# Key and value projections as one product, indexer query groups between the key steps, masks and table edges on GpSimd

## The chip, the cores and the metric

One core of a Trainium2 chip runs the whole program in one launch. The metric is the device time of the run in microseconds (us). The kernel before: 1031.42 us, median of 3 runs (1030.24 to 1037.22).

## The reference

One inference step of a transformer layer for a prompt of 512 tokens and a sample of 32 tokens that sees 512 cached ones; the model width is 1024.

```python
h = rmsnorm(x, g_attn)
qa, ka, va, qb, kb, vb, iq, ik, iw, ga, gb = split(h @ w_in)
# a: window attention over chunks c-2..c, with a sink per head, 8 heads on 2 key heads
oa = softmax([qa @ ka.T / 8 + bias, sink]) @ va
# b: sparse attention: an indexer scores all keys, the best of them are attended to
score = sum_h iw[h] * relu(iq[h] @ ik.T) * scale
sel = top_k(score, 128 for the prompt, 136 for the sample)
ob = softmax(qb @ kb[sel].T / 8 + bias) @ vb[sel]
x = x + (sigmoid(ga) * (oa @ w_branch_a) + sigmoid(gb) * (ob @ w_branch_b)) @ w_out
x = x + moe(rmsnorm(x))        # 32 experts of 512, two per token
x = x + sigmoid(rmsnorm(x) @ w_ple_gate) * (p @ w_ple)
y = rmsnorm(x)
# outputs: y, and the new ka, va, kb, vb, ik of prompt and sample
```

`bias` is a T5 relative position table, turned into one row per distance (a Toeplitz table).

## The kernel before

The program is written engine by engine: each engine has its own list of instructions, and semaphores (`x.wait_ge(sem, n)`, `.then_inc(sem, n)`) are all that orders them between engines. SyncE (`sp`) issues nearly all DMAs, in program order, on one queue; GpSimd (`pool`) stores the new keys and values. The stages around the change, in TensorE's order:

1. The normed rows are turned (L900) and VectorE scales them with `g_attn` into hT, 8 planes of 128 features by 544 tokens (512 prompt, 32 sample).
2. Indexer queries: `project` (L881) multiplies slab 0, the 512 indexer columns of `w_in`, by hT in four groups `('iq', m)` of 128 columns, in full f32. In the profile one such product appears as two instructions: 64 products are x128.
3. Indexer keys and head weights: `by_token` (L888), five token tiles, 72 columns, into two narrow PSUM slots, which VectorE copies out (L1894, L1896). The keys are turned (L920 for the prompt, L925 and L926 for the sample).
4. Dots (L940 for the prompt's blocks 1 to 3, eight heads each; L936 for the sample). ScalarE applies the relu (L1522) and VectorE sums over the heads (L1914, L1917).
5. Key and value projections, branch b, then branch a (L952): each of five token tiles is 24 products of 256 columns. Between them stand `sums` (L959), which adds up the sample's four partial scores, and the transposes of the keys (L964, L969, L970).
6. Attention queries `qb` and `qa` (L980): four groups of 48 products each, 272 columns.
7. Attention over 80 units (`scores_of_two`, L1014, and on), from which the later stages follow: merge, output, routing, experts, the last gate.

From step 5 on, a product with f32 accuracy is made of three single-pass ones (fp32r): an operand v is split into a high part (`high`, ScalarE, L1490, a copy rounded to fp32r) and a low part, v minus high (`low_of` L743, `low` L758, GpSimd), and the product is high x high + high x low + low x high. `hT_f` and `hT_lo` are the parts of hT. `sw_high` and `sw_split` count the high and low parts of weights, `f_high` and `f_split` those of hT.

PSUM is shared by two rings, `WIDE` (three slots of two banks) and `NARROW` (two slots of one bank). A list gives the order of their uses and the engine that reads each out; `open_slot` makes TensorE wait for the use three (or two) before, `close` makes the reader wait for TensorE.

Slab 0 holds the indexer weights and later the `qb` weights. Slab 1 is loaded in pieces: `slab_ikw` (indexer keys) and `slab_kva` both start at its beginning, `slab_kvb` lies in its second half, and the `qa` weights fill it at the end. So the load of `slab_kva` waits for the last reader of `slab_ikw`.

SyncE's order is: x, three gains, the bias table's inputs, slabs iq, ikw and kvb, the caches, the constants; then, after `tabp_ready`, the write of the spread bias table to DRAM (`toeplitz<-arena`, 3 MB); then slab `qb` after the last indexer query, slab `kva` after the prompt's indexer keys are turned, slab `qa` after the last of branch a's projections, and ten loads that bring the table back as `toep_a`, `toep_b`, `toep_sa` and `toep_sb`.

VectorE picks the highest scores, eight at a time (`next_eight` L1933, `take_eight` L1937, which overwrites what it took with TAKEN): 16 rounds for each prompt block, 10 for the sample before attention. `mask` (L1944) writes -BIG where a score isn't TAKEN. Behind the selection VectorE writes the edges of the tables: two strips of `toep_a` that no query may see (L1959, L1960) and the sinks (L1961, L1963). Then it clears four PSUM columns (L1966, L1967) after the last attention query was evicted, and `toep_ready` lets attention start.

Of the kernel before, what the change touches and what calls it, by code (L numbers as in the profile page):

```python
# [32 lines left out]
P = 128  # L33
# [14 lines left out]
KV = 2  # L48
# [28 lines left out]
CONSTS = 6  # L77
# [44 lines left out]
def ring(uses, slots):  # L122
# [23 lines left out]
    + [(('kvb', t), 'act') for t in range(TILES)] + [(('kva', t), 'act') for t in range(TILES)], 2)  # L146
# [78 lines left out]
def _program(nc, A, ctx):  # L225
# [53 lines left out]
    for lo, hi in ((0, 16), (16, 24), (24, 32), (32.5, 40.5), (40.5, 48.5), (48.5, 56.5), (68.5, 73), (80, 97), (97.25, 114.25)):  # L279
        twin(arena, "front", int(lo * 256), int(hi * 256))  # L280
# [34 lines left out]
    hT_lo = at(114.25, [KD, NT])  # L315
    score = hb[:, 0:3 * (PAST + NS)].rearrange("p (b n) -> p b n", b=3)
# [23 lines left out]
    kv_hi = {'b': at(32.5, [KD, 256]), 'a': at(40.5, [KD, 256])}  # L340
# [133 lines left out]
    consts_in, gains_in = sem("consts_in"), sem("gains_in")  # L474
# [64 lines left out]
    def _(sp):  # L539
# [7 lines left out]
        for n, g in enumerate(['g_attn', 'g_ffn', 'g_ple']):  # L547
            load(gains[:, n, :], A[g][0].rearrange("(p c) -> p c", c=KD), gains_in)
# [19 lines left out]
        load(sink_in[:, :], A['attn_sink'].to_broadcast([P, HEADS]), consts_in)  # L568

        sp.wait_ge(tabp_ready, 1)  # L570
# [145 lines left out]
    def _(pool):  # L716
# [32 lines left out]
        pool.wait_ge(sw_high, 1)  # L749
        low_of(slab_kvb, slab_kvb, kv_hi['b'], "front").then_inc(sw_split, 1)  # L750

# [8 lines left out]
        pool.wait_ge(sw_high, 2)  # L760
        low(slab_kva, kv_hi['a'], "front").then_inc(sw_split, 1)

# [6 lines left out]
        query_weights_low(3, slab[0], qb)  # L769
        pool.wait_ge(narrow_out['act'], NARROW[('kvb', 4)].out)  # L770
# [3 lines left out]
        pool.wait_ge(narrow_out['act'], NARROW[('kva', 4)].out)  # L774
# [5 lines left out]
        link(pool.memset(toep_sb[:, :, 0:PAST - WIN], 0.0))  # L780
        link(pool.memset(ones, 1.0))

        query_weights_low(7, slab[1], qx)

        def spread_inverse(s):

# [1653 lines left out]
```

## Time and profile before

| what | before |
|---|---|
| median of 3 runs | 1031.42 us (1030.24 to 1037.22) |
| the profiled execution's own time | 1036.8 us |
| its span | 1035.0 us |
| mean granted clock of TensorE | 0.967 of full |
| TensorE busy | 925.9 us |
| VectorE busy | 378.2 us |
| ScalarE busy | 256.5 us |
| GpSimd busy | 132.4 us |

The profile is of one execution, and its span leaves 1.8 us of that execution's time out. Starts are counted from the span's start. "PE" is TensorE, "DVE" VectorE, "ACT" ScalarE, "POOL" GpSimd, "SPq" SyncE's queue of DMA issues; L940 is line 940 of the kernel. The span of an issue ends when it is handed over, not when its data has landed; the DMA view gives the time to landing. The granted clock is a share of 2.4 GHz, so 0.5 is 1.2 GHz.

### The profile page before, as it was taken

To read this page: it belongs to the slowest core of one execution; us is meant where nothing else is said; L and a number is where in the kernel's file an instruction comes from. 1 tells how busy PE (TensorE), PEld (TensorE's weight loads), DVE (VectorE), ACT (ScalarE), POOL (GpSimd) and SP (SyncE) were. 2 spreads that over 40 slices of the span, in tenths; PEclk is the share of its full clock that TensorE was granted. 3 is DMA by queue.
4 is the path that set the end of the run, shared out by engine and by line. 5 is a ranking of instruction groups with operands and counts; after the bars stand their busy time and mean duration, and the time that the engine had idled before them with its cause. 6 is when DMAs were issued, how large, how long until landed. Compare 5 with 4: busy or idle time off the path is not lost.

```text
span 1035.0 us, 14155 instructions
## 1 busy us (share of the span) xinstructions
PE 925.9 (89%) x5699; PEld 591.2 (57%) x5702; DVE 378.2 (37%) x974; ACT 256.5 (25%) x523; POOL 132.4 (13%) x136
## 2 busy tenths in 40 slices
PE   7989999999999999998999977877887888887996
PEld 7869995456999998994333322322322222234775
DVE  4179996764233436453111101101101011102796
ACT  6244326764323233221000000000000000001542
POOL 2403701113030000001111110011010110000000
PEclk9999998999999999997999999999999899999998
DMA  9850602002834316366999999999999999996601
GB/s 265 118 152 2 203 1 62 1 2 68 263 105 120 78 46 244 128 236 239 427 427 425 427 428 428 424 428 425 429 426 426 427 426 425 427 428 264 254 22 66
DMA packets 60132, 263.72 MB, mean 255 GB/s; under 512 B 11054, under 2 KB 36030, under 8 KB 46224
## 3 DMA queue, kind: packets, MB, share of 16 engines
q1 hardware_dynamic: 54160, 250.99, 63.0%
q0 software_dynamic: 5296, 9.79, 2.6%
q10 hardware_dynamic: 624, 2.23, 0.6%
q8 instruction: 36, 0.59, 0.2%
q14 instruction: 16, 0.13, 0.0%
HBM read 253.99 MB, written 16.85 MB: 262 GB/s over the span
## 4 chain that ended last, share of the span: by engine, by line
PE 63%; DMA 29%; DVE 4%; ACT 2%; issue 1%; SPq 1%; DVEq 0%; ACTq 0%
DMA arena<-in_w_up 25%; PE ps L1111 13%; PE ps L1278 12%; PE ps L980 5%; PE ps L1143 4%; PE ps L1426 4%; PE ps L1303 3%; PE ps L881 3%; PE ps L952 3%; DMA arena<-in_w_ple 2%; PE ps L1044 2%; PE ps L1014 2%; PE ps L1065 2%; PE ps L1399 1%; PE ps L1172 1%
## 5 line engine op out<-in xcount | busy, mean ns | idle before, releaser
L1278 PE MATMUL ps<-arena,hT 128*64 128x512 f32 x960 | 234.5, 641 | 39.4 <-DMA arena<-in_w_up 39.2
L1278 PEld LDWEIGHTS ps<-arena,hT 128*64 128x64 f32 x960 | 71.6, 141 | 199.3 <-issue 149.4
L2211 DVE TENSOR_TENSOR xf<-xf,ps 128x256 f32<-128x256 f32 x32 | 13.5, 421 | 401.6 <-ACT xf L1699 379.1
L1111 PE MATMUL ps<-arena_merge,arena_merge 128*128 128x256 f32 x624 | 99.7, 287 | 0.0
L1303 PE MATMUL ps<-arena,xf 128*64 128x512 f32 x336 | 76.7, 598 | 12.8 <-DVE xf L2214 12.8
L1111 PEld LDWEIGHTS ps<-arena_merge,arena_merge 128*128 128x128 f32 x624 | 87.4, 188 | 0.0
L836 POOL DMA_INDIRECT expert_rows<-xf,arena x32 | 32.2, 1007 | 425.6 <-ACT xf L1703 399.8
L1111 PE MATMUL ps<-xf_merge,arena_merge 128*128 128x256 f32 x480 | 82.0, 288 | 0.0
L1699 ACT ACTIVATE xf<-ps 128x256 f32<-128x256 f32 x30 | 11.6, 385 | 259.1 <-PE ps L1278 259.1
L1111 PEld LDWEIGHTS ps<-xf_merge,arena_merge 128*128 128x128 f32 x480 | 69.3, 188 | 0.0
L1703 ACT ACTIVATE xf<-ps 128x512 f32<-128x512 f32 x30 | 17.9, 598 | 159.8 <-PE ps L1303 159.8
L1303 PEld LDWEIGHTS ps<-arena,xf 128*64 128x64 f32 x336 | 24.3, 136 | 50.8 <-issue 43.0
L1143 PE MATMUL ps<-arena_merge,arena_merge 128*128 128x256 f32 x304 | 49.0, 286 | 1.2 <-DVE arena_merge L2045 1.0
L1303 PE MATMUL ps<-hT,xf 128*64 128x512 f32 x176 | 40.2, 598 | 6.6 <-DVE xf L2214 5.2
L1426 PE MATMUL ps<-arena_gate,hT_gate 128*128 128x512 f32 x192 | 44.4, 391 | 1.1 <-ACT arena L1741 0.6
L1143 PEld LDWEIGHTS ps<-arena_merge,arena_merge 128*128 128x128 f32 x304 | 42.9, 191 | 2.5 <-DVE arena_merge L2045 2.0
L980 PE MATMUL ps<-xf_merge,arena_front 128*128 128x272 f32 x256 | 42.9, 289 | 0.0
L2045 DVE TENSOR_TENSOR arena_merge<-arena,arena_merge 128x256 fp32r<-128x256 f32 (+2 forms) x34 | 39.9, 1228 | 5.1 <-ACT arena_merge L1490 5.0
L1490 ACT ACTIVATE arena_merge<-arena 128x256 fp32r<-128x256 f32 (+3 forms) x43 | 37.1, 919 | 16.2 <-DMA arena<-in_w_branch_a 7.2
L1426 PEld LDWEIGHTS ps<-arena_gate,hT_gate 128*128 128x128 f32 x192 | 35.8, 188 | 9.1 <-ACT arena L1741 1.0
L980 PEld LDWEIGHTS ps<-xf_merge,arena_front 128*128 128x128 f32 x256 | 36.2, 189 | 0.0
L1559 ACT ACTIVATE hT<-ps 128x256 f32<-128x256 f32 (+3 forms) x64 | 25.0, 394 | 21.9 <-PE ps L1044 21.2
(309 smaller groups left out, 1311.1 us busy)
## 6 DMA issues: line engine op xcount, KB each, us to landing
arena<-in_w_gate SPq DMA_DIRECT2D x30, 2048.0 KB, 29.4
arena<-in_w_up SPq DMA_DIRECT2D x30, 2048.0 KB, 37.0
arena<-in_w_down SPq DMA_DIRECT2D x11, 2048.0 KB, 36.4
hT<-in_w_down SPq DMA_DIRECT2D x11, 2048.0 KB, 36.5
arena<-in_w_down SPq DMA_DIRECT2D x20, 1024.0 KB, 32.2
arena<-in_w_in SPq DMA_DIRECT2D x10, 1024.0 KB, 6.2
arena<-in_w_in SPq DMA_DIRECT2D x3, 2048.0 KB, 10.5
arena<-in_w_gate SPq DMA_DIRECT2D x8, 512.0 KB, 9.0
```

Source lines behind the costliest of these rows:

```text
L836: pool.indirect_dma_start(ys, bass.IndirectOffsetOnAxis(ap=of, axis=0), src, None, bounds_check=row_bound, oob_is_err=False).then_inc(s, 16)
L881: mm = pe.matmul(w[:, a * 512:a * 512 + HALF], lhs(c), hT[:, c, a * HALF:(a + 1) * HALF], start=c == 0, stop=c == KD - 1)
L952: mm = pe.matmul(ps[0:ROWS[t], 6 + slot, 0:256], rounded(st[:, c, tok(t)]), rounded(mv[:, c, :], "front"), start=c == 0 and k == 0, stop=c ...
L980: mm = pe.matmul(w[:, a * 512:a * 512 + HALF], rounded(st, "front"), rounded(mv[:, c, a * HALF:(a + 1) * HALF]), start=c == 0 and k == 0, ...
L1111: mm = pe.matmul(w[:, 2 * lo_t:lo_t + hi_t], rounded(st[:, c, cols]), rounded(mv[:, c, lo_t:hi_t]), start=c == 0 and k == 0, stop=c == pla ...
L1143: mm = pe.matmul(w[:, q * QW:(q + 1) * QW], rounded(st[t // 2][:, t % 2, m, :]), rounded(mv[:, m, :]), start=m == 0 and k == 0, stop=m == ...
L1278: mm = pe.matmul(ps[g * BLK:(g + 1) * BLK, 2 + s, :], xsT[:, c, col:col + BLK], expert_columns(k, slice(0, 2), c, g), start=c == 0, stop=c ...
L1303: mm = pe.matmul(ps[g * BLK:(g + 1) * BLK, 6 + s, :], hidT[s][:, c % 2, c // 2 * BLK:(c // 2 + 1) * BLK], dn_at(k, c)[:, g * 512:(g + 1) * ...
L1426: mm = pe.matmul(w[:, cols], rounded(st[:, c, :], "gate"), rounded(mv[:, c, cols], "gate"), start=c == 0 and k == 0, stop=c == KD - 1 and ...
L1490: return act.activation(rounded(dst, stage), src, ACT.Copy)
L1559: act.activation(pT_sb[k2][:, j % 2, 0:tiles, j // 2 % 2, :], ps[:, 4 + u % 2, 0:tiles * P].rearrange("p (k n) -> p k n", n=P), ACT.Copy)\
L2045: return dve.tensor_tensor(rounded(v, stage), v, rounded(hi, stage).bitcast(F32), ALU.subtract)
```

## The change

- Indexer queries: group 0 stays in full f32. Groups 1, 2 and 3 are made of three single-pass products, with the weights' high parts `iq_hi` (ScalarE, three instructions, ahead of kvb's) and low parts (GpSimd, in place in slab 0). TensorE's order becomes: group 0, indexer keys, group 1, the prompt's keys turned, group 2, the sample's keys turned, group 3, dots.
- ScalarE waits for slab `kva` and splits it between the sample's indexer keys and group 3's eviction; before, it did so after the dots.
- SyncE issues slab `kva` after the last indexer key tile, ahead of slab `qb`. The gains `g_ffn` and `g_ple` move from the program's start to behind the constants, ahead of the table write.
- Branch a's and b's key and value columns become one product of 512 moving columns: 5 tiles of 24 instead of twice 5 of 24. All four transposes follow the last tile. ScalarE copies each tile in two halves, and the high parts of the `qb` weights are made ahead of these copies.
- `sums` stands behind the second tile, and ScalarE copies it out instead of VectorE.
- The masks of the prompt's blocks 1 to 3 are written by GpSimd (`selected` counts VectorE's finished blocks), block 1's after the qb parts, block 2's after the stores, block 3's after the qa parts.
- The table edges and sinks are written by GpSimd, after block 2's mask and ahead of the qa weights' low parts. Attention's start waits for both GpSimd and VectorE (`toep_ready` 2), ScalarE's first exp for four masks.

```diff
-    [(('xT', t), 'dve') for t in range(TILES)] + [(('iq', m), 'dve') for m in range(4)]
-    + [(('ikT', s), 'dve') for s in 'ps']
-    + [(('dots', b, h), 'act') for b in BLOCKS for h in range(KV if b == 's' else HEADS)] + [('sums', 'dve')]
+    [(('xT', t), 'dve') for t in range(TILES)] + [(('iq', 0), 'dve'), (('iq', 1), 'dve'), (('ikT', 'p'), 'dve')]
+    + [(('iq', 2), 'dve'), (('ikT', 's'), 'dve'), (('iq', 3), 'dve')]
+    + [(('dots', b, h), 'act') for b in BLOCKS for h in range(KV if b == 's' else HEADS)] + [('sums', 'act')]
...
+        sp.wait_ge(narrow_full, NARROW[('ikw', 4)].fill)
+        load(slab_kva, w_in[:, :, C_KVA:C_KVA + 256], slab_in['kva'])
         sp.wait_ge(wide_full, WIDE[('iq', 3)].fill)
         load(slab[0], w_in[:, :, C_QB:C_QB + 512], slab_in['qb'])
-        sp.wait_ge(wide_full, WIDE[('ikT', 'p')].fill)
-        load(slab_kva, w_in[:, :, C_KVA:C_KVA + 256], slab_in['kva'])
-        sp.wait_ge(narrow_full, NARROW[('kva', 4)].fill)
+        sp.wait_ge(narrow_full, NARROW[('kv', 4)].fill)
         load(slab[1], w_in[:, :, C_QA:C_QA + 512], slab_in['qa'])
...
+        mask(2)
+        pool.wait_ge(toep_moved, 16 + 16 * 10)
+        pool.wait_ge(consts_in, 16 * CONSTS)
+        pool.wait_ge(masks_ready, 3)
+        link(pool.memset(toep_a[0:CHUNK, :, TW - CHUNK:TW], -BIG))
+        link(pool.memset(toep_a[CHUNK:P, :, 0:CHUNK], -BIG))
...
+        pool.sem_inc(toep_ready, 1)
         link(pool.memset(ones, 1.0))
 
-        query_weights_low(7, slab[1], qx)
+        query_weights_low(10, slab[1], qx)
+        mask(3)
...
+        def index_queries(m):
+            w = wide(open_slot(WIDE, ('iq', m), wide_out))
+            pe.wait_ge(f_split, KD)
+            for k in range(3):
+                if k == 2:
+                    pe.wait_ge(sw_split, m)
+                for c in range(KD):
+                    st = slab[0][:, c, m * P:(m + 1) * P] if k == 2 else iq_hi[m][:, c, :]
+                    mv = hT_lo if k == 1 else hT_f
+                    for a in range(2):
+                        mm = pe.matmul(w[:, a * 512:a * 512 + HALF], rounded(st, "front"),
+                                       rounded(mv[:, c, a * HALF:(a + 1) * HALF]),
+                                       start=c == 0 and k == 0, stop=c == KD - 1 and k == 2)
+            mm.then_inc(wide_full, 1)
...
+        pe.wait_ge(sw_split, 5)
+        for t in range(TILES):
+            slot = open_slot(NARROW, ('kv', t), narrow_out)
+            for c in range(KD):
+                for k, (st, mv) in enumerate(((hT_f, kv_hi2), (hT_f, kv_lo2), (hT_lo, kv_hi2))):
+                    mm = pe.matmul(by_half(ps[0:ROWS[t], 6 + slot, :]), rounded(st[:, c, tok(t)]), rounded(mv[:, :, c, :], "front"),
+                                   start=c == 0 and k == 0, stop=c == KD - 1 and k == 2)
+            mm.then_inc(narrow_full, 1)
+            if t == 1:
+                sample_sums()
...
+        index_queries(0)
+        index_queries(1)
+        index_keys('p', 0, NP)
+        index_queries(2)
+        index_keys('s', NP, PAST + NS)
+        act.wait_ge(slab_in['kva'], 16)
+        high(kv_hi['a'], slab_kva, "front").then_inc(sw_high, 1)
+        index_queries(3)
```

ScalarE from the high parts of hT to the dots' relus, before. `xf_merge` are hT's high parts, `arena_front<-arena` splits a weight slab, `64x544` evicts half a group of indexer queries, `128x512` and the second `128x544` the indexer keys, `hT<-ps` is a relu.

```order
L1490 ACTIVATE xf_merge_68<-hT 128x544 x8
L1490 ACTIVATE arena_front_81<-arena 128x2048
L1503 ACTIVATE arena_front_85<-ps 64x544 x8
L1507 ACTIVATE arena_front_83<-ps 128x512
L1507 ACTIVATE arena_front_83<-ps 128x544
L1522 ACTIVATE hT<-ps 128x256 x8
```

The same place in the changed kernel, with the same names.

```order
L1537 ACTIVATE xf_merge_68<-hT 128x544 x8
L1537 ACTIVATE arena_front_84<-arena 128x1024 x3
L1537 ACTIVATE arena_front_80<-arena 128x2048
L1553 ACTIVATE arena_front_83<-ps 64x544 x4
L1558 ACTIVATE arena_front_81<-ps 128x512
L1553 ACTIVATE arena_front_83<-ps 64x544 x2
L1558 ACTIVATE arena_front_81<-ps 128x544
L1537 ACTIVATE arena_front_80<-arena 128x2048
L1553 ACTIVATE arena_front_83<-ps 64x544 x2
L1582 ACTIVATE hT<-ps 128x256 x8
```

Three weight splits stand ahead of kvb's, and kva's split (the second `128x2048`) now stands ahead of the last group's eviction; before it stood behind all relus.

SyncE around the table write, before. `128x8x512` is slab qb, then qa; `128x8x256` is slab kva.

```order
L541 DMA g_fin<-in_g_final 128x1024
L541 DMA sink_in<-in_attn_sink 128x8
L541 DMA toeplitz<-arena 2048x1x384
L541 DMA arena<-in_w_in 128x8x512
L541 DMA arena<-in_w_in 128x8x256
L541 DMA arena<-in_w_in 128x8x512
L541 DMA arena<-toeplitz 128x8x256 x2
```

And in the changed kernel.

```order
L543 DMA g_fin<-in_g_final 128x1024
L543 DMA sink_in<-in_attn_sink 128x8
L543 DMA gains<-in_g_ffn 128x8
L543 DMA gains<-in_g_ple 128x8
L543 DMA toeplitz<-arena 2048x1x384
L543 DMA arena<-in_w_in 128x8x256
L543 DMA arena<-in_w_in 128x8x512 x2
L543 DMA arena<-toeplitz 128x8x256 x2
```

Slab kva comes right behind the table write, ahead of slab qb, and two gain loads stand ahead of the write.

## Rows read from the trace of the kernel before

**Rows 1.** the page: the chain that ended last, share of the span by engine.
```profile
PE 63%; DMA 29%; DVE 4%; ACT 2%; issue 1%; SPq 1%; DVEq 0%; ACTq 0%
```

**Rows 2.** the chain of waits, 20 to 161 us: start, length, engine, line, count.
```profile
20.68 29.53 PE ps L881 x128
50.20 8.23 PE ps L888 x80
...
58.95 0.64 PE ps L920 x4
...
60.95 0.74 DVE arena_front L1900
61.73 0.52 PE ps L940 x2
...
79.63 14.31 PE ps L952 x120
...
111.99 48.51 PE ps L980 x384
160.52 0.62 ACT arena L1549
```

**Rows 3.** ScalarE's timeline: start, length, line, operation, count.
```profile
20.56 4.49 ACT L1490 ACTIVATE xf_merge<-hT 128x544 fp32r<-128x544 f32 x8 [3.56 <-DVE hT L1856]
24.96 1.89 ACT L1490 ACTIVATE arena_front<-arena 128x2048 fp32r<-128x2048 f32 x1
28.24 1.25 ACT L1503 ACTIVATE arena_front<-ps 64x544 fp32r<-64x544 f32 x2 [1.39 <-PE ps L881]
```

**Rows 4.** SyncE's queue: start and length of each issue.
```profile
4.08 0.44 SPq L541 DMA_DIRECT2D gains<-in_g_ple  x1
...
25.37 0.68 SPq L541 DMA_DIRECT2D toeplitz<-arena  x1
...
50.24 0.57 SPq L541 DMA_DIRECT2D arena<-in_w_in  x1
...
59.61 0.54 SPq L541 DMA_DIRECT2D arena<-in_w_in  x1
...
111.14 13.15 SPq L541 DMA_DIRECT2D arena<-toeplitz  x10
```

**Rows 5.** DMA issues in 25:26, 50:52, 59:60, us to landing; the packets of 50:52.
```profile
toeplitz<-arena SPq DMA_DIRECT2D x1, 3072.0 KB, 33.7
...
DMA packets 132, 0.20 MB, mean 101 GB/s; under 512 B 0, under 2 KB 132, under 8 KB 132
...
arena<-in_w_in SPq DMA_DIRECT2D x1, 2048.0 KB, 14.4
...
arena<-in_w_in SPq DMA_DIRECT2D x1, 1024.0 KB, 7.7
```

**Rows 6.** the chain, the kernel's last product, 512 columns moving.
```profile
1003.86 21.81 PE ps L1426 x96
```

**Rows 7.** GpSimd's timeline.
```profile
22.03 10.42 POOL L743 TENSOR_TENSOR arena_merge<-hT,xf_merge 128x544 fp32r<-128x544 f32 x8 [19.13 <-DVE arena L1878]
...
121.43 10.07 POOL L758 TENSOR_TENSOR arena_front<-arena,arena_front 128x512 fp32r<-128x512 f32 x8 [5.24 <-ACT arena_front L1490]
```

**Rows 8.** VectorE's timeline: mask, sample's copy, selection's end, last edge row.
```profile
97.66 0.29 DVE L1944 TENSOR_SCALAR arena<-hT 128x256 bf16<-128x256 f32 x1
97.87 0.70 DVE L1955 COPY xf<-ps 32x544 f32<-32x544 f32 x1
...
158.37 0.70 DVE L1937 MATCH_REPLACE8 xf<-nrm,xf 32x544 f32<-32x544 f32 x1
...
160.44 0.67 DVE L1963 TENSOR_SCALAR arena<-sink_in 32x2 f32<-32x2 f32 x4
```

**Rows 9.** windows: busy time by engine, granted clock, DMA share, GB/s.
```profile
62.00:66.00 4.00, 3.94 (x19) 3.71 (x19) 3.58 (x10) 2.87 (x8) 0.00 (x0) 0.59 0.96 333
...
165.00:170.00 5.00, 4.94 (x17) 2.11 (x17) 2.88 (x14) 3.48 (x17) 1.98 (x2) 0.51 0.58 145
```

More of the change, by code:

```diff
@@ L145 @@
     [('table', 'dve')] + [(('ikw', t), 'dve') for t in range(TILES)]
-    + [(('kvb', t), 'act') for t in range(TILES)] + [(('kva', t), 'act') for t in range(TILES)], 2)
+    + [(('kv', t), 'act') for t in range(TILES)], 2)
 UNITS, GROUP_OF, GROUP_UNITS, SET_OF, SET_LAST = [], [], [], [], []
@@ L767, in query_weights_low, with mask @@
                 low(s[:, 4:8, m * P:(m + 1) * P], q_hi(dst, m, 1), "front").then_inc(sw_split, 1)
-        query_weights_low(3, slab[0], qb)
-        pool.wait_ge(narrow_out['act'], NARROW[('kvb', 4)].out)
+        query_weights_low(6, slab[0], qb)
+        def mask(b):
+            _, keys, sc = block_score(b)
+            m0, _ = MSK[b]
+            pool.wait_ge(selected, b)
+            pool.tensor_scalar(msk[:, m0:m0 + keys], sc, TAKEN, -BIG, ALU.is_gt, ALU.mult).then_inc(masks_ready, 1)
+        mask(1)
+        pool.wait_ge(narrow_out['act'], NARROW[('kv', 4)].out)
         for nm, c in (('new_k', 0), ('new_v', P)):
@@ L909, in _ @@
         pe.wait_ge(wide_out['dve'], WIDE[('xT', 4)].out)
-        for m in range(4):
-            slot = open_slot(WIDE, ('iq', m), wide_out)
-            project(slot, lambda c: slab[0][:, c, m * P:(m + 1) * P], P, None, 0).then_inc(wide_full, 1)
+        slot = open_slot(WIDE, ('iq', 0), wide_out)
+        project(slot, lambda c: slab[0][:, c, 0:P], P, None, 0).then_inc(wide_full, 1)
         pe.wait_ge(slab_in['ikw'], 16)
@@ L1495, in _, with index_queries @@
             high(hT_f[:, c, :], hT[:, c, 0:NT]).then_inc(f_high, 1)
+        act.wait_ge(slab_in['iq'], 16)
+        for m in range(1, 4):
+            high(iq_hi[m], slab[0][:, :, m * P:(m + 1) * P], "front").then_inc(sw_high, 1)
         act.wait_ge(slab_in['kvb'], 16)
         high(kv_hi['b'], slab_kvb, "front").then_inc(sw_high, 1)
-        for m in range(4):
+        def index_queries(m):
             w = wide(close(WIDE, ('iq', m), wide_full))
@@ L1523, in _ @@
                 n += 1
-        act.wait_ge(slab_in['kva'], 16)
-        high(kv_hi['a'], slab_kva, "front").then_inc(sw_high, 1)
-        for br, dst, past in (('b', kbT, PAST), ('a', kaT, WIN)):
-            kv_n = kv_b if br == 'b' else kv_a
-            for t in range(TILES):
-                slot = NARROW[('kv' + br, t)].slot
-                act.wait_ge(narrow_full, NARROW[('kv' + br, t)].fill)
-                act.activation(kv_n[0:ROWS[t], t, :], ps[0:ROWS[t], 6 + slot, 0:256], ACT.Copy)\
-                    .then_inc(narrow_out['act'], 1)
+        act.wait_ge(slab_in['qb'], 16)
+        query_weights_high(slab[0], qb)
+        for t in range(TILES):
+            slot, r = close(NARROW, ('kv', t), narrow_full), ROWS[t]
+            act.activation(kv_b[0:r, t, :], ps[0:r, 6 + slot, 256:512], ACT.Copy)
+            act.activation(kv_a[0:r, t, :], ps[0:r, 6 + slot, 0:256], ACT.Copy).then_inc(narrow_out['act'], 1)
+            if t == 1:
+                w = wide(close(WIDE, 'sums', wide_full))
+                act.activation(score_s[0:NS, :], w[0:NS, 0:PAST + NS], ACT.Copy).then_inc(wide_out['act'], 1)
+        for br, dst, past in (('b', kbT, PAST), ('a', kaT, WIN)):
             w = wide(close(WIDE, ('k' + br + 'T', 'p'), wide_full))
@@ L1879, in _, with index_queries @@
         dve.memset(msk, 0.0)
-        for m in range(4):
+        def index_queries(m):
             w = wide(close(WIDE, ('iq', m), wide_full))
@@ L1941, in mask @@
             m0, _ = MSK[b]
-            for lo in range(0, P, 32) if b == 's' else (0,):
+            for lo in range(0, P, 32):
                 ins = dve.tensor_scalar(msk[lo:lo + rows, m0:m0 + keys], sc, TAKEN, -BIG, ALU.not_equal, ALU.mult)
```

107 lines of the change are left out of this document (55 added, 52 removed).

## The prediction, made before the changed kernel ran

> **What bounds the kernel now.** I read the page's chain first: TensorE holds 63% of it, and where it is not TensorE it is mostly a DMA [rows 1]. The change touches the first 165 us alone, so I followed the chain of waits through them [rows 2]. The reader is to see one unbroken TensorE path: indexer queries (L881, 29.53 us), indexer keys (L888, 8.23), a short relay over ScalarE and VectorE that ends at 60.95 + 0.74, the dots from 61.73, the first of two key and value products at 79.63 (L952, 14.31 for 120 products; the second is as long), the attention queries from 111.99 (L980, 48.51), and attention after 160.52. All later stages, expert weights included, are started by TensorE's own progress, so what is won or lost before 160 us should arrive at the end whole. Then I read the three other engines for slack, and SyncE's queue, because the change moves a load past another one [rows 4, 5].
>
> **Indexer queries: what TensorE saves.** Before, one of four groups costs 29.53 / 4 = 7.38 us [rows 2]. Three groups now become 48 single-pass products each. The same shape (272 columns, 128x128 weights) runs in L980 at 48.51 / 384 = 0.126 us [rows 2], so a group costs 6.06 and three save 3 x 1.32 = 4.0 us of TensorE time.
>
> Against that stands a small stall. ScalarE now makes three high parts of the indexer weights before it evicts group 0. It is at 25.05 when f_high is done [rows 3]; three parts of 1024 elements at half of 1.89 bring it to 27.9, the key/value part (1.89) to 29.8, the eviction (1.25) to 31.0 [rows 3], and VectorE's two subtractions (0.74 each by the row of 60.95) to 32.6. VectorE takes the key tiles only after that, and with two slots TensorE's third tile waits about 1.5 us. So group 0 ends at 28.1, the keys at 28.1 + 8.2 + 1.5 = 37.8, and three groups (18.2) with two sets of transposes (0.64 each) end at 57.3. GpSimd's low parts are in time: 22.03 + 10.42 = 32.45 for hT, then 1.25 per 512 elements [rows 7], so 2.5 us per group, the first at 35, needed at 41.8, the last at 40, before its group starts.
>
> **Indexer queries: what sets the end.** TensorE's saving would let the dots start at 57.3 + 1.25 + 1.48 + 0.1 = 60.1 to 60.4, against 61.73: 1.3 to 1.6 us earlier. It does not get that far. ScalarE now waits for slab kva and splits it (1.89) ahead of evicting group 3; the load is issued after the last key tile, at 38, into SyncE's queue behind the bias table's write to DRAM. That write was issued at 25.37 and took 33.7 us to land, at 59.1 [rows 4, 5]. The queue does not overtake: the 2 MB load issued at 50.24 took 14.4 us, until 64.6, and of the 132 packets seen in 50 to 52 us none was of 2 KB, the size of its rows; all are the table's 1.5 KB [rows 4, 5]. After the write it needed 64.6 - 59.1 = 5.5 us, and the 1 MB load behind it (59.61 + 7.7 = 67.3) 2.7 more [rows 4, 5].
> The Trainium skill (DMA: Bandwidth & Descriptors, Queues, rings and completion order) says that descriptors of one ring are consumed in ring order; the trace agrees by the 132 packets. It adds that completion isn't ordered over a queue, which would let kva land early only on engines done with the table.
>
> In the changed kernel the two gain loads (0.44 and 0.45; row of 4.08) stand ahead of the table write, so it goes out at 26.3 and lands at 60.0; kva lands at 60.0 + 2.7 = 62.7. ScalarE: split until 64.6, eviction of group 3 until 65.9; VectorE's subtractions until 67.4; dots at 67.5. That is +5.8 us against 61.73. TensorE idles from 57.3 for 10 us, and its 4 us of saving and the 1.5 us stall both vanish in it. Bounds: if the load slips through, -1.5; if it lands with the slowest ring and a further delay, +7.
>
> TensorE's clock is the second price. After a stretch with little TensorE work 62 to 66 shows 0.59 and then full speed, while 165 to 170 is at 0.51 [rows 9]: the 1.2 GHz level. The dots paid this before as well, and VectorE's sums paced them, so I add nothing; the upper bound is the rival below. The skill (TensorE: Matmul & The Clock Gate, What's actually happening) says that the 1.2 GHz level follows an idle spell and ends with sustained work; rows 9 agree, and by that rule too nothing is added unless the gaps in the dots hold it down.
>
> **Joined key and value product.** 240 products of 256 columns (2 x 14.31 = 28.6 us) become 120 of 512. The nearest row is the kernel's last product: 21.81 / 96 = 0.227 us at 512 columns [rows 6], so 27.3 us: -1.3. No loss of one product's fixed cost would give 0, so the bounds are -1.4 and 0. The second ScalarE copy ahead of the transposes costs 0.3, and a wait between the two branches goes, 0.2. Taken: -1.3. Splitting the qb weights (eight ScalarE parts) moves ahead of the copies, but lies in the 5 us before the first tile is full.
>
> **Masks, sums and edges.** VectorE drops three masks (0.21 from the first to the next row, about 0.8 in all), the sums copy (0.74) and the edges (159.1 to 161.1) [rows 8]. In the old trace the edges ended 0.2 us after ScalarE's first half of the last eviction (160.52 + 0.62) and before the second [rows 2, 8]: hidden. Gone, they win nothing, since attention waits for that eviction. They do give cover: VectorE's selection, shifted by +5.8 - 1.5, ends at 163.4, before the new end of qa at 165.
> On GpSimd seven edge instructions now stand ahead of the low parts of the qa weights and wait for the last bias table load. Those loads were issued from 111.14 to 124.3 [rows 4]; the last are small and land within the 7.7 us of a 1 MB load [rows 5], by 132.0 at the latest; the new ones follow the join's end, +3.3, so 135.3. The edges cost 2 us by VectorE's rows (159.1 to 161.1), 8.8 by GpSimd's 1.25 each [rows 7, 8]; small as they are I take 2.5. The first qa part (2.5) is then ready by 140.3 at the latest, and TensorE wants it at 67.5 + 17.9 + 31.1 + 24.3 = 140.8 (dots 61.73 to 79.63; join to queries 32.4 - 1.3; half of 48.51). Cost 0; with 8.8 for the edges it would be 5.8 late, which is the upper bound. The last mask comes after these parts, but VectorE's selection of block 3 is the later one, and attention wants it at 165.
>
> **Sum.** +5.8 - 1.3 + 0 = +4.5 us. On the profiled execution (1036.8) that gives 1041.3; on the median of the runs, 1031.4, it gives 1035.9. About 1% (10 us) is what a measurement of this kernel can tell from no change, so this is a small loss inside it.
>
> **The rivals.**
> A. The kva load isn't held by the table write, or lands on early rings by 52, so the reordered indexer pays: -1.5 and -1.3, so 1028.6. For it: rings finish at different times, and 1 MB is small. Against it: no large packet in 50 to 52 us [rows 5].
> B. Slower by more than 1%: after 10 us without work TensorE comes back at 1.2 GHz and the gappy dots hold it there. Place: 67 to 86 us. Dots and the sample's part take 17.9 us with the clock back after some 4 us; with it low throughout, about half as much more, +8; if it also catches 5 us of the joined product, +2.5. Time 1031.4 + 4.5 + 8 = 1044. It decides if the clock is still at 0.5 beyond 73 us. For it, 165 to 170 [rows 9]; against it, 66 us, where it came back although VectorE paced the dots.
> C. GpSimd is late: edges cost 8.8 us, or the table's copies land later, and TensorE waits at the qa weights, up to 5.8 us by the bound above; taken at 3: 1039.
> D. The main story holds, but TensorE's 512-column products gain nothing: 1037, inside the forecast.
>
> **How the numbers follow.** Forecast with D 0.66, A 0.18, B 0.07, C 0.07, anything else 0.02. The range for 8 in 10 runs from near A's value to C's and past: 1028.5 to 1041. Only B gives more than +1%, and A gives less than -0.3%; for a deeper gain no row speaks. Faster by over 1% 0.03, within 1% 0.90, slower by over 1% 0.07.
>
> **What would show it.** Right: slab kva lands near 62 to 63 us; ScalarE's wait ahead of the second 2048-element split ends with a DMA; TensorE's dots start at 67 to 68 after 10 us idle; the indexer groups take 6.1 us; L1002 takes 27.3 us for 120; qa starts without a wait; its last eviction starts 4 to 5 us later than at 160.52. Wrong: dots before 62 us, a kva load that took under 15 us, a wait of TensorE for GpSimd near 140, or a late stage whose length changed.

## The result, and the profile after

The changed kernel takes 1046.06 us, median of 4 runs (1044.94 to 1046.73), against 1031.08 us, median of 4 runs of the kernel before (1030.24 to 1037.22). The ratio of the runs on record is 1.0114 (95% interval 1.008 to 1.0148), the plain quotient of the two medians 1.0145; by either it is slower, by 1 to 1.5%. The forecast was 1035.9, range 1028.5 to 1041.

The two medians need one remark. The kernel before scatters: three of its first four runs lie near 1030.8 and one at 1037.2, and of 25 runs in a later job the median is 1036.36 (1028.91 to 1037.78). Against those the changed kernel is 9.7 us slower. The profiled executions, 1036.8 us before and 1045.66 us after, differ by 8.9 us, and so do their spans, so the traces are compared at 8.9.

The page of the changed kernel: span, busy time by engine, and the chain that ended last by engine.

```profile
span 1043.9 us, 14025 instructions
...
PE 927.7 (89%) x5627; PEld 587.8 (56%) x5630; DVE 377.5 (36%) x963; ACT 259.1 (25%) x527; POOL 146.2 (14%) x149
...
PE 59%; DMA 31%; DVE 4%; ACT 3%; issue 1%; SPq 1%; DVEq 0%; ACTq 0%
```

TensorE is busy 1.8 us longer, and DMAs now hold 31% of the chain, 29% before [rows 1]. The new share is one load in the first 65 us: 23.1 of 1043.9 us are 2.2%. The chain of the changed kernel (start, length, what), with lines that answer to [rows 2]:

```profile
32.64 7.25 PE ps L914 x48
...
39.91 23.12 DMA arena<-in_w_in
...
63.05 1.91 ACT arena_front L1537
...
70.85 0.50 DVE hT L1980
...
87.64 11.33 PE ps L1002 x48
...
100.00 16.88 PE ps L1002 x72
...
119.73 48.51 PE ps L1027 x384
...
169.90 0.51 PE ps L1061 x4
```

L914 are key tiles 3 to 5, L1537 ScalarE's split of slab kva, L1980 VectorE's first weighted sum of the dots, L1002 the joined product, L1027 the attention queries, L1061 attention. The reader is to see the 23.12 us of a load in the middle. TensorE works on indexer groups 1 to 3 beside it for the first 20 us and then stands idle until the dots:

```profile
67.72 2.97 PE L984 MATMUL ps<-arena_front,arena_front 128*128 128x256 f32 x12 [7.55 <-DVE arena_front L1945]
```

The joined product starts at 87.64, 79.63 before: +8.0. The queries start at 119.73, 111.99 before: +7.7. Attention starts at 169.90 and 162.06: +7.8.

SyncE's queue and the landing of slab kva, which answer to [rows 4, 5]:

```profile
26.26 0.68 SPq L543 DMA_DIRECT2D toeplitz<-arena  x1
39.91 0.57 SPq L543 DMA_DIRECT2D arena<-in_w_in  x1
...
arena<-in_w_in SPq DMA_DIRECT2D x1, 1024.0 KB, 23.1
```

The load goes out at 39.91 and lands 23.1 us later, at 63.0. Alone behind a free queue a load of this size lands in about 6 us (run e2_table_behind_kva below).

VectorE between the last subtraction of indexer group 3 and the first weighted sum: the four copies together, the first of them by itself, and the same four in the trace before:

```profile
66.21 1.46 DVE L1945 TENSOR_TENSOR arena_front<-ps,arena_front 64x544 fp32r<-64x544 f32 x2 [9.24 <-ACT arena_front L1553]
67.69 2.74 DVE L1971 COPY nrm<-x_nat 32x2 f32<-32x2 f32 x4
...
67.69 1.89 DVE L1971 COPY nrm<-x_nat 32x2 f32<-32x2 f32 x1
...
61.59 0.66 DVE L1905 COPY nrm<-x_nat 32x2 f32<-32x2 f32 x4
```

The four copies of 32x2 take 2.74 us; before they took 0.66. They were not all slowed: the first took 1.89 us, until 69.58, the second and third 0.16 each, as before, and the fourth 0.49.

GpSimd's work that is new or moved, to be read against [rows 7, 8]:

```profile
65.04 4.52 POOL L749 TENSOR_TENSOR arena_front<-arena,arena_front 128x2048 fp32r<-128x2048 f32 x1 [21.45 <-ACT arena_front L1537]
...
105.79 1.11 POOL L782 TENSOR_SCALAR arena<-hT 128x256 bf16<-128x256 f32 x1 [6.18 <-DVEq L2018]
...
126.00 1.50 POOL L782 TENSOR_SCALAR arena<-hT 128x384 bf16<-128x384 f32 x1 [0.70 <-DVEq L2018]
137.40 0.52 POOL L799 MEMSET arena<- 64x512 f32 x1 [9.89 <-DMA arena<-toeplitz]
...
140.43 10.06 POOL L769 TENSOR_TENSOR arena_front<-arena,arena_front 128x512 fp32r<-128x512 f32 x8
150.57 1.95 POOL L782 TENSOR_SCALAR arena<-hT 128x512 bf16<-128x512 f32 x1
```

The low part of slab kva runs from 65.04 to 69.56: VectorE's first copy ended 0.02 us behind it. The masks take 1.11, 1.50 and 1.95 us, the seven edge instructions and their waits 2.8 us (137.40 to 140.19). The first two low parts of the qa weights end near 143.0, and TensorE wants them near 144.0, when half of its 48.5 us from 119.73 are over: a spare of 1 us.

Granted clock (the first number behind the five busy times) in the changed kernel, at the key tiles, the dots and attention's start:

```profile
34.00:37.00 3.00, 3.00 (x20) 3.00 (x19) 0.36 (x2) 0.00 (x0) 3.00 (x3) 0.63 0.91 103
37.00:40.00 3.00, 3.00 (x21) 2.67 (x21) 0.45 (x3) 0.00 (x0) 3.00 (x2) 0.50 0.89 101
...
70.00:74.00 4.00, 2.83 (x11) 2.47 (x10) 3.74 (x9) 1.92 (x5) 1.05 (x2) 0.50 0.15 35
...
170.00:175.00 5.00, 4.44 (x24) 2.63 (x25) 2.40 (x18) 3.52 (x17) 1.04 (x1) 0.63 1.02 295
175.00:180.00 5.00, 5.00 (x18) 2.17 (x18) 3.52 (x14) 2.84 (x12) 1.04 (x1) 0.50 0.10 18
180.00:190.00 10.00, 9.95 (x48) 4.21 (x47) 6.25 (x24) 7.83 (x25) 2.08 (x2) 0.75 0.00 1
```

### The profile page after: what moved, and what is told of

Same layout as the page of the kernel before. It is cut to its first block, busy times and chain, and to the rows that moved or that the text cites. A ratio compares the mean times of both kernels' runs of the same rounds, so it can differ in the third digit from the quotient of the medians.

```text
span 1043.9 us, 14025 instructions
## 1 busy us (share of the span) xinstructions
PE 927.7 (89%) x5627; PEld 587.8 (56%) x5630; DVE 377.5 (36%) x963; ACT 259.1 (25%) x527; POOL 146.2 (14%) x149
## 3 DMA queue, kind: packets, MB, share of 16 engines
q1 hardware_dynamic: 54160, 250.99, 62.8%
## 4 chain that ended last, share of the span: by engine, by line
PE 59%; DMA 31%; DVE 4%; ACT 3%; issue 1%; SPq 1%; DVEq 0%; ACTq 0%
DMA arena<-in_w_up 25%; PE ps L1158 13%; PE ps L1325 12%; PE ps L1027 5%; PE ps L1190 4%; PE ps L1473 4%; PE ps L1350 3%; PE ps L1002 3%; DMA arena<-in_w_ple 2%; DMA arena<-in_w_in 2%; PE ps L1061 2%; PE ps L1091 2%; PE ps L1112 2%; PE ps L1446 1%; PE ps L1219 1%
## 5 line engine op out<-in xcount | busy, mean ns | idle before, releaser
L1027 PE MATMUL ps<-xf_merge,arena_front 128*128 128x272 f32 x256 | 42.9, 289 | 0.0
L1537 ACT ACTIVATE arena_merge<-arena 128x256 fp32r<-128x256 f32 (+3 forms) x43 | 37.1, 918 | 19.2 <-DMA arena<-in_w_branch_b 9.1
L1473 PEld LDWEIGHTS ps<-arena_gate,hT_gate 128*128 128x128 f32 x192 | 35.8, 188 | 9.1 <-ACT arena L1800 1.0
L1027 PEld LDWEIGHTS ps<-xf_merge,arena_front 128*128 128x128 f32 x256 | 36.2, 189 | 0.0
## 6 DMA issues: line engine op xcount, KB each, us to landing
arena<-in_w_down SPq DMA_DIRECT2D x20, 1024.0 KB, 31.2
```

Source lines behind the costliest of these rows:

```text
L1027: mm = pe.matmul(w[:, a * 512:a * 512 + HALF], rounded(st, "front"), rounded(mv[:, c, a * HALF:(a + 1) * HALF]), start=c == 0 and k == 0, ...
L1473: mm = pe.matmul(w[:, cols], rounded(st[:, c, :], "gate"), rounded(mv[:, c, cols], "gate"), start=c == 0 and k == 0, stop=c == KD - 1 and ...
L1537: return act.activation(rounded(dst, stage), src, ACT.Copy)
```

## The experiments

Times are medians; "before" is the kernel before on the same chip in the same job.

| run | us | ratio to before, interval |
|---|---|---|
| e1_before_again | 1037.11 | 1.0003 (0.9986 to 1.002) |
| e2_table_behind_kva | 1039.13 | 1.003 (1.0011 to 1.005) |
| e3_low_after_copies | 1046.43 | 1.0101 (1.0084 to 1.0118) |
| e4_kva_loaded_early | 1038.24 | 1.0022 (1.0009 to 1.0034) |
| e5_kvb_split_later | 1033.88 | 0.9975 (0.9958 to 0.9992) |
| e6_columns_side_by_side | 1033.71 | 0.9982 (0.996 to 1.0004) |
| e7_masks_edges_vector | 1044.82 | 1.0084 (1.0048 to 1.012) |
| e8_kept_busy | 1031.7 | 0.9961 (0.9943 to 0.9978) |
| e9_before_kept_busy | 1032.68 | 0.9974 (0.9958 to 0.9991) |
| e10_busy_in_the_gap | 1030.48 | 0.9948 (0.9932 to 0.9965) |

**The kernel before, a second profile.** No edit.

> The kernel before, unchanged, for a second profile of it. The profile before was of an execution of 1036.8 us, the other runs but one lie near 1030.5, and the changed kernel lies 15 us above these but its profile only 8.9 us above the profile before. Theory A (the kernel before has two modes of a clock that comes back late): an execution near 1030.5 shows about 6 us less in one stage, with TensorE at half clock for about that much less time; attention's start (160 to 180 us) or the router (460 to 485 us) are the candidates. Rival B: the 6 us lie in the DMA-bound expert stage, spread over 600 to 950 us, with the clock the same.

The execution that was profiled took 1028.84 us, 8.0 less than the first profile's. Its windows, to be held against 165 to 170 in [rows 9]:

```profile
165.00:170.00 5.00, 4.70 (x30) 2.41 (x31) 4.25 (x19) 4.78 (x22) 1.04 (x1) 1.00 0.29 58
170.00:175.00 5.00, 5.00 (x32) 2.36 (x30) 4.31 (x14) 4.87 (x15) 2.08 (x2) 1.00 0.02 5
```

The clock is at 1.00 where it was at 0.51 before. From attention's first scores to the merge's first gate product it takes 85.0 us (160.8 to 245.8), in the first profile 89.0 (162.1 to 251.0). Attention starts 1.3 us earlier too. These 1.3 us are there at the first indexer query: from 10 to 20 us the clock was 1.00, in the first profile 0.83. The stages behind attention are 2.7 us shorter: 1.1 between the merge and the experts' first product, where the clock stood at 0.50 for 10.2 us (from 461 us on) against 13.7 us (from 465), and 1.4 in the stage from 947 to 958 us, whose cause stays open. So theory A holds for half of the difference at the place that it names first, and the clock was lower in the slow execution at three places in all.

**The table write behind slab kva.**

```diff
-        sp.wait_ge(tabp_ready, 1)
-        load(toep_d, ...)
         sp.wait_ge(narrow_full, NARROW[('ikw', 4)].fill)
         load(slab_kva, ...)
+        sp.wait_ge(tabp_ready, 1)
+        load(toep_d, ...)
```

> The changed kernel with the bias table's write to DRAM issued behind slab kva's load instead of ahead of it; nothing else. Theory A (kva is held by the table write in SyncE's queue, and ScalarE's wait on it sets the dots): kva lands at 43 to 47 us instead of 63.0, dots start near 60.5 instead of 67.7, GpSimd's low part of kva ends before VectorE's copies, attention starts 9 us earlier than in the changed kernel: about 1037. Rival B (the wait isn't what costs; the loss is the clock or the joined product): no more than 3 us gained: 1043 to 1046.

1039.13 us, 6.9 under the changed kernel. Slab kva lands 5.9 us after its issue at 41.14, and the wait is gone from the chain:

```profile
32.59 8.52 PE ps L914 x48
41.11 7.33 PE ps L952 x48
...
64.60 7.62 PE ps L984 x30
```

But the dots start at 64.6, not at 60.5. The first two lines say why: the last three key tiles took 8.52 us, and the indexer group behind them 7.33 instead of 6.1. The granted clock was 0.50 from 34 to 40 us and 0.55 from 40 to 44. So the load was the cause that bound the changed kernel, and right behind it a second one stood, which it had covered. The copies take 0.69 us here: GpSimd's low part of kva ran from 58.71 to 63.28 and was over before them.

**GpSimd's low part after VectorE's copies.**

```diff
         pool.wait_ge(sw_high, 5)
+        pool.wait_ge(relu_used, 1)
         low_of(slab_kva, slab_kva, kv_hi['a'], "front").then_inc(sw_split, 1)
```

> The changed kernel, but GpSimd starts the low part of slab kva only after VectorE's first weighted sum. Theory A (VectorE's four 32x2 copies were held by GpSimd's tensor operation, 2.74 us instead of 0.66): the copies take 0.7 us again, the first weighted sum starts at 68.8 instead of 70.9, the time falls by 2.0 us: 1044. Rival B (the copies were slow for another reason, a semaphore or the DMA landing in x_nat's neighbourhood): copies still at 2.7 us, no change.

1046.43 us: no gain where 2 us were expected, though the copies did what theory A said. VectorE (columns: start, length, line, operation, count):

```profile
67.77 0.68 DVE L1972 COPY nrm<-x_nat 32x2 f32<-32x2 f32 x4
...
69.71 7.75 DVE L1984 SCALAR_TENSOR_TENSOR hT<-hT,x_nat 128x256 f32<-128x256 f32 x7
...
78.33 4.54 DVE L1984 SCALAR_TENSOR_TENSOR hT<-hT,x_nat 128x384 f32<-128x384 f32 x7
```

GpSimd in the same stretch, and from the chain the longest of VectorE's weighted sums:

```profile
69.82 4.75 POOL L749 TENSOR_TENSOR arena_front<-arena,arena_front 128x2048 fp32r<-128x2048 f32 x1 [26.29 <-DVE hT L1981]
...
70.23 4.63 DVE hT L1984
```

The copies take 0.68 us again, and the first weighted sum starts at 69.19 instead of 70.85. The seven sums behind it, of 256 columns, which read two operands from SBUF, now take 7.75 us, where 7 x 0.52 = 3.6 is their time in the trace before; those of 384 columns, behind the end of GpSimd's operation, take their usual 4.54. Again one instruction took all of it: the sum at 70.23 lasted 4.63 us and ended at 74.86, 0.3 behind GpSimd's operation, and the other six took 0.5 each. So VectorE was not slowed by a share: one instruction was held until GpSimd's operation was over. The cost went from a copy to a sum and grew to 4.1 us, since GpSimd now started together with the sums and not 2.7 us ahead of the copies. Two kinds of instructions were not held. In the changed kernel VectorE's subtractions (66.21, 1.46) read one operand from PSUM and kept their time, with GpSimd busy all the while; in the kernel before the same GpSimd operation (82.20 to 86.81) lay beside five rounds of the selection, which took their usual 0.43 and 0.41 us each. The Trainium skill (GPSIMD Engine Reference, Specifications) says that GpSimd shares its SBUF interfaces with VectorE and contends with instructions in a two-port mode or with two SBUF inputs; the sums (two SBUF inputs) and the subtractions (one operand in PSUM) agree. The copies have one input; whether they ran in a two-port mode no run here shows.

**Slab kva loaded early.** The place of its own costs 2.25 KB per partition, where the bias tables of the sample come later.

```diff
-    slab_ikw = at(16, [KD, IKW])
+    slab_ikw = at(56.75, [KD, IKW])
...
         load(slab_kvb, ...)
+        load(slab_kva, ...)
...
-        sp.wait_ge(narrow_full, NARROW[('ikw', 4)].fill)
-        load(slab_kva, ...)
```

> The changed kernel with slab ikw in a place of its own, so that slab kva needs no reader to end and is loaded right behind slab kvb, ahead of the table write. Theory A: ScalarE doesn't wait for kva, dots start near 60.5 (before: 61.7), the joined product and the transposes win 0.3, attention starts 1.5 us earlier than in the kernel before: 9.5 us under the changed kernel in the profile, and 0.998 of the kernel before if the stages behind are equal. Rival B (a second cause of about 6 us exists that only the medians show): it stays 5 us or more above the kernel before, 1036.

1038.24 us, 7.8 under the changed kernel and still 0.2% above the kernel before. ScalarE doesn't wait for the load, and dots start at 62.8. The second cause is now in the open. TensorE's key tiles, first two and last three:

```profile
27.52 3.69 PE L913 MATMUL ps<-arena,hT 128*128 128x72 f32 x32
32.31 7.69 PE L913 MATMUL ps<-arena,hT 128*128 128x72 f32 x48 [1.10 <-DVE x_nat L1961]
```

and the granted clock:

```profile
34.00:37.00 3.00, 3.00 (x16) 3.00 (x16) 0.36 (x2) 0.00 (x0) 3.00 (x2) 0.50 0.90 101
37.00:40.00 3.00, 3.00 (x22) 2.67 (x21) 0.36 (x2) 0.00 (x0) 3.00 (x2) 0.50 0.93 103
```

TensorE waits 1.10 us for VectorE, which is late because ScalarE split slab kvb ahead of evicting group 0. From 34 us on the clock is at 0.50, the 1.2 GHz level, for 6 us and more, and the three tiles take 7.69 us, where at full clock about 4.5 is left for them (8.23 for all five [rows 2] less the 3.69 of the first two). The changed kernel, e2_table_behind_kva, e3_low_after_copies and e7_masks_edges_vector have the same wait of 1.10 us and the same fall of the clock.

**Slab kvb split after the eviction.**

```diff
-        act.wait_ge(slab_in['kvb'], 16)
-        high(kv_hi['b'], slab_kvb, "front").then_inc(sw_high, 1)
...
         index_queries(0)
+        act.wait_ge(slab_in['kvb'], 16)
+        high(kv_hi['b'], slab_kvb, "front").then_inc(sw_high, 1)
         index_queries(1)
```

> Run e4_kva_loaded_early with one more move: ScalarE evicts indexer group 0 before it splits slab kvb, not after. In that run TensorE waited 1.1 us before the third key tile, and the granted clock then stood at 0.50 from 34 to 40 us. Theory A (the wait of 1.1 us made the clock fall, and both cost 4 to 5 us): no wait, clock 1.00 from 31 to 44 us, the 80 key products take 8.2 us, dots start at 57.5 to 58.5 instead of 62.8; 4 to 5 us less, 1033 to 1034, below the kernel before. Rival B (the clock falls there by itself, because the mix of small products is too thin): the wait goes, but the clock still falls; 1 us gained.

1033.88 us, 4.4 less than e4_kva_loaded_early and 0.25% under the kernel before. The chain:

```profile
29.75 8.22 PE ps L913 x80
37.97 6.21 PE ps L951 x48
...
60.34 0.81 PE ps L983 x2
```

and its windows:

```profile
34.00:37.00 3.00, 3.00 (x30) 2.93 (x30) 0.47 (x3) 0.00 (x0) 3.00 (x2) 1.00 0.91 102
37.00:40.00 3.00, 3.00 (x32) 2.90 (x30) 0.60 (x4) 0.00 (x0) 3.00 (x2) 1.00 0.89 100
165.00:170.00 5.00, 5.00 (x20) 2.00 (x18) 3.31 (x12) 3.28 (x15) 1.04 (x1) 0.50 0.30 61
170.00:175.00 5.00, 5.00 (x21) 2.07 (x17) 2.17 (x8) 3.53 (x12) 0.00 (x0) 0.50 0.00 0
```

All 80 key products take 8.22 us without a gap, and the clock is 1.00 from 34 to 40. Dots start 22.4 us after the end of the key tiles (37.97 to 60.34). In this execution the clock had been at 0.67 from 20 to 28 us, and the indexer's group 0 took 9.80 us for 7.4, so the keys started 2.3 us late and the dots at 60.3, past the 58.5 that was expected. Run e8_kept_busy has the same front and started its keys at 27.5, as e4_kva_loaded_early did, at full clock: its keys ended at 35.8 against 40.0, and its dots started at 58.1 against 62.8. Rival B is out: in the five profiled executions with the wait the clock fell to 0.50 between 34 and 40 us, in the four without it (this run, e6_columns_side_by_side, e8_kept_busy, e10_busy_in_the_gap) it stayed at 1.00. A wait of 1.1 us cost four, itself included.

**Columns side by side.**

```diff
-    kv_lo2, kv_hi2 = at(16, [2, KD, 256]), at(32.5, [2, KD, 256])
+    kv_lo2, kv_hi2 = at(16, [KD, 2, 256]), at(32.5, [KD, 2, 256])
```

with `slab_kva`, `slab_kvb` and the two high parts as its halves.

> Run e5_kvb_split_later with the key and value columns of both branches laid side by side in memory, so that the 512 moving columns of the joined product are contiguous instead of two pieces 8 KB apart. In the changed kernel such a product took 0.235 us; the last product of the kernel, contiguous, takes 0.227. Theory A (the jump between the two pieces costs about 8 ns in each): 0.227, 27.3 us for 120, 0.9 us less. Rival B (the difference has another source, such as weight loads of another kind): 0.235 again, same time as that run.

1033.71 us, no difference. That is the median of ten runs of which one took 2288 us, for a reason that isn't known; without it the median is 1033.56. The joined product in two pieces:

```profile
76.59 11.33 PE ps L1001 x48
...
88.95 16.88 PE ps L1001 x72
```

11.33 / 48 and 16.88 / 72 are 0.235 us each, as in the changed kernel. The jump between the pieces costs nothing. Why these products take 0.235 and those of the last stage 0.227 [rows 6] stays open.

**Masks and edges back on VectorE.**

```diff
-        mask(2)
-        pool.wait_ge(toep_moved, 16 + 16 * 10)
...
-                dve.sem_inc(selected, 1)
+                mask(b)
...
+        dve.wait_ge(toep_moved, 16 + 16 * 10)
+        dve.memset(toep_a[0:CHUNK, :, TW - CHUNK:TW], -BIG)
```

> The changed kernel with the prompt's masks and the table edges back on VectorE; the sample's sums stay with ScalarE. Theory A (this part neither wins nor costs, both sides lie beside TensorE): attention starts within 0.5 us of the changed kernel's 169.9, VectorE ends the edges before ScalarE's last eviction; 1046, within 0.3%. Rival B (GpSimd's masks and edges slow VectorE's selection, or hold the qa weights): 1 to 3 us faster than the changed kernel.

1044.82 us (5 runs, 1040.92 to 1046.64), 1.2 us under the changed kernel's median; three of the five lie below the fastest of its four (1044.94), so by the times alone the 1 us of rival B isn't excluded. The traces decide it for the part in question: from the first dot to attention's start it takes 102.1 us (68.3 to 170.4), in the changed kernel 102.2 (67.7 to 169.9). VectorE ends the edges at 169.0, and the columns are cleared at 170.18, after ScalarE's last eviction: covered, as before. Theory A holds up to attention's start; where the 1.2 us lie, if they are real, is not shown.

**Idle products at attention's start.** To e5_kvb_split_later:

```diff
+        def keep_busy(n):
+            for _ in range(n):
+                pe.matmul(ps[:, 7, 0:P], ident[:, :], ident[:, :], start=True, stop=True)
+
+        keep_busy(6)
         scores_of_two(0)
...
+            if u == LAG:
+                keep_busy(9)
```

> Run e5_kvb_split_later with 15 products of the identity by itself into an unused bank at attention's start: six behind the last query projection, nine ahead of the first turn. They compute nothing that is used. In the second profile of the kernel before (1028.8 us) the clock stayed at 1.00 through 165 to 175 us, in the first (1036.8) it stood at 0.50, and attention took 85.0 against 88.9 us. Theory A (TensorE's gaps there let the clock fall, and that is the scatter of the kernel before): clock 1.00 from 160 to 185, attention 85 us, all runs near the fastest, 4 us below e5_kvb_split_later. Rival B (the products are themselves in the way, or too few): same or slower, clock at 0.5 as before.

1031.7 us, 2.2 less than e5_kvb_split_later, half of what was expected. The clock stayed at 1.00 from 160 to 185, but the first six products stood behind TensorE's wait for the last eviction and took 1.5 us of their own. From attention's start (159.6) to the merge it took 86.7 us, 1.7 more than in the second profile of the kernel before with the same clock. Nine idle products lie in that stretch; by the 1.5 us of six they are an estimated 2.3 us of work, but that they are the reason isn't shown.

**The same in the kernel before.** The six now stand ahead of that wait.

```diff
+        keep_busy(6)
         for by in ('dve', 'act'):
             pe.wait_ge(wide_out[by], WIDE_DONE[by])
...
+            if u == LAG:
+                keep_busy(9)
```

> The kernel before with 15 products of the identity that are used by nobody: six behind the last query projection, ahead of TensorE's wait for its eviction, nine ahead of attention's first turn. Theory A (the kernel before has its scatter of 1029 to 1038 us from the clock, which falls in these two gaps in most executions): attention takes 85 to 86 us instead of 88.9, most runs at 1030 to 1034, median 3 us below the kernel before. Rival B (the scatter comes from elsewhere, such as the DMA-bound stage): runs spread as before, no gain.

1032.68 us (1031.66 to 1036.28), 2.9 under the kernel before in the same job. The windows of its profiled execution, the slowest of ten at 1036.28 us:

```profile
20.00:28.00 8.00, 8.00 (x24) 6.09 (x24) 1.31 (x3) 5.76 (x9) 7.39 (x6) 0.64 0.74 173
165.00:170.00 5.00, 4.56 (x36) 3.45 (x35) 2.31 (x18) 3.26 (x16) 1.04 (x1) 1.00 1.05 298
```

Attention is at full clock (1.00 from 170 to 175 us too) and takes 86.5 us. Eight of the ten runs lie in the 1030 to 1034 of theory A. This execution was slow for another reason, which the first line shows: 0.64 in 20 to 28 us, at the first indexer queries, and its dots started at 63.7. So attention's start is not the only place where this program may or may not lose its clock: the first products are another, and only the first of the two was mended.

**And in the version without waits.** e8_kept_busy with the six products moved in the same way.

> Run e8_kept_busy with its first six idle products ahead of TensorE's wait for the last eviction instead of behind it, where they took 1.5 us themselves. Theory A: attention starts 1.5 us earlier against the last query product (2 instead of 3.3 us behind it), the clock stays at 1.00, 1 to 1.5 us less than in that run: 1030.4. Rival B (the clock is held only if the products stand right ahead of attention): the clock falls, attention takes 88 us or more, 1033.

1030.48 us (4 runs, 1029.04 to 1030.98), ratio 0.9948 to the kernel before. It is the fastest kernel of this study, 15.6 us under the changed kernel. Attention starts 1.7 us after the end of the last query product (156.2 to 157.8), in e8_kept_busy 3.0 (156.6 to 159.6), and the clock holds, from 170 to 175 us too:

```profile
165.00:170.00 5.00, 4.70 (x30) 2.11 (x28) 4.13 (x15) 4.78 (x18) 0.99 (x2) 1.00 0.00 0
```

## Why the prediction was wrong

**Right: the mechanism that set the front.** The prediction said that slab kva would queue behind the table write and land at 62.7, that ScalarE's wait would set the dots, and that they would start at 67.5. They landed at 63.0 and started at 67.7. Run e2_table_behind_kva shows that the order in the queue is the cause: with that alone undone, kva lands 5.9 us after its issue and 6.9 us are back. Rival A had 0.18 and is out.

**Wrong: what stands between the dots and the joined product.** The step "dots at 67.5. That is +5.8 us" took the start of the dots as what counts and left out who reads them. VectorE makes four copies first, and GpSimd's low part of kva, put in the same 5 us by the same late load, holds the first of them until it ends: 2.74 us for the four instead of 0.66. The first weighted sum starts at 70.85 against 62.84, 8.0 later and not 5.8. From the first dot to that sum it takes 3.1 us, with the copies free 1.4 (e2_table_behind_kva, e3_low_after_copies), so the hold is 1.7 us of the missing 2. The other 0.3 go with the clock: where the dots started at full clock it took 1.1 us (before, e4_kva_loaded_early). e3_low_after_copies shows the contention by moving it onto a sum. The prediction moved GpSimd's operation without asking what VectorE does beside it; before, it lay beside the selection, which it didn't hold.

**Rival B: its sign came, its price didn't.** The prediction said that a low clock would decide for B if it was still at 0.5 beyond 73 us. It was at 0.50 until about 75.7 us. But from the first weighted sum to the joined product it takes 16.79 us in both traces: VectorE paced the dots at either clock, and the product ran at 1.00. That the measured time lies near B's 1044 is chance.

**Wrong in size: the joined product.** Taken at 0.227 per product, it measured 0.235 (28.2 us for 120), 28.7 before. That wins 0.45, and what lies between the products and behind them, up to the queries, grew by 0.2. From the start of the product to the start of the queries it takes 32.1 us, 32.4 before: -0.3 and not -1.3. Why such a product takes longer here than in the last stage isn't shown. It lies inside the bounds of -1.4 and 0, nearer the end that rival D stood for.

**Right: masks, edges and sums win and cost nothing.** e7_masks_edges_vector shows it for masks and edges, up to attention's start. The prediction read the old edges as ending 0.2 us after ScalarE's first half of the last eviction; they end at 161.11, just before its end at 161.14, which changes nothing. The estimate of 2.5 us for the edges was near the 2.8 measured. They started at 137.4, when the last table load was in, 2.1 us past the time that was called the latest. The masks took 1.1 to 2.0 us on GpSimd and were not priced at all; only 1 us was to spare at the qa weights.

**Half right: the stall at the key tiles.** It was forecast at 1.5 us and taken as vanishing in the wait for kva. It measured 1.1 us, and it did vanish there, in the changed kernel: TensorE still idles 7.55 us before the dots, not 10, since the stall took the clock with it and the last three key tiles took 7.25 us for about 4.5. But the 60.1 to 60.4 us at which "TensorE's saving would let the dots start" without the load was wrong by 2.4 to 4.5 us (62.8 in e4_kva_loaded_early, 64.6 in e2_table_behind_kva). The clock was weighed at the dots alone, where VectorE sets the pace and it costs little, and not at the keys, where TensorE itself does.

**The account at 8.9 us.** 5.98 until the last subtraction (61.69 to 67.67), 2.03 for the held copy and the first dots, -0.27 for the product and the transposes, 0.10 at the last eviction, 0.99 from attention's start to the merge (89.97 against 88.98 us), where the clock was low from about 172 to 185 us, some 3 us longer than before, and 0.07 in all stages behind. Together 8.9. The forecast was 4.5, so the copy and the first dots (2.0), the product (1.0), attention (1.0) and 0.4 in small pieces are what it lacked.

**Wrong in the base.** The forecast set its 4.5 us on the median, 1031.4. Of the 10.2 us between 1035.9 and 1046.06 the missing effect is 4.4; 5.4 are this base, and 0.4 lie between the changed kernel's profiled execution and its median. The profile it was worked out from was of an execution of 1036.8, and the prediction named both without asking what lies between them. In the two profiles of that kernel, 8.0 us apart, half is the clock at attention's start (e1_before_again, e9_before_kept_busy). All four runs of the changed kernel lie within 1.8 us, none 6 us below the rest. Set on 1036.8, even the forecast's own sum gives 1041.3, past the range. Why none of the changed kernel's four runs was a fast one is not shown: only one was profiled.

## What to carry to other kernels

A load that is issued earlier in the program isn't earlier on the chip if the queue already holds a long transfer: add up what stands in the queue, and where the wait for the load stands in the consumer's own list. Move an operation on GpSimd only after looking at what VectorE does beside it: here a copy and a two-input sum from SBUF were held until GpSimd's operation ended, subtractions with a PSUM operand and the selection were not, so what counts is how much of GpSimd's operation is still to run. And a wait of 1 us on TensorE, where TensorE is the bound, can cost several, since the clock may go with it: it cost four here. A few products that nobody uses, placed in such a gap at attention's start, were worth 3 us.

## What the runs showed of the hardware that was not expected

- A TensorE wait of 1.10 us at 31.2 us was followed by a granted clock of 0.50 from 34 to 40 us and more; the same products without the wait ran at 1.00. e4_kva_loaded_early and e5_kvb_split_later differ by one moved ScalarE instruction, and five executions with the wait stand against four without it. The Trainium skill (TensorE: Matmul & The Clock Gate, "A second HAM failure mode: psum-queue depth-cycling") says that frequent short idle spells of TensorE between groups of products make its clock go back and forth, at a loss of throughput. These runs agree in direction, and they add that one such spell can be enough.
- One GpSimd operation of 4.5 us held a single VectorE instruction until its own end: a copy of 0.16 us took 1.89, and when the operation was moved, a weighted sum of 0.52 took 4.63. The instructions behind it kept their time, but for the fourth copy (0.49 us), whose reason isn't known. In e7_masks_edges_vector, where the same two lie side by side, the copies took 2.74 us again.
- The same kernel ran between 1028.8 and 1038.4 us, 1%, and its two profiled executions differ in where TensorE's clock was low: at 165 to 175 us (0.5 or 1.00), at 10 to 20 us (0.83 or 1.00) and at the routing (0.50 for 13.7 or 10.2 us). At 20 to 28 us it was 1.00 in both, 0.64 in e9_before_kept_busy and 0.67 in e5_kvb_split_later.
- A single-pass product of 512 columns took 0.235 us in one stage and 0.227 in another, with contiguous columns in both.
